# Norm scales in a two-block transformer on one core: roots and reciprocals in place of powers on GpSimd, and the weight splits around the feed-forward norms in another order

## The reference, cut to what matters

```python
def rmsnorm(x, g):
    return x * lax.rsqrt(jnp.mean(x * x, axis=-1, keepdims=True) + 1e-6) * g

def first_block(x, ...):                       # layer 0: attention, layer 1: recurrence
    for layer in range(2):
        h = rmsnorm(x, norm_mix_pre[layer])
        m = attention_mixer(h, ...) if layer % 2 == 0 else recurrent_mixer(h, ...)
        x = x + rmsnorm(m, norm_mix_post[layer])
        h = rmsnorm(x, norm_ffn_pre[layer])
        f = (silu(h @ w_gate[layer]) * (h @ w_up[layer])) @ w_down[layer]
        x = x + rmsnorm(f, norm_ffn_post[layer])

def second_block(x, ...):                      # no norm behind the sublayers
    h = h + dilated_diff_mixer(rms_norm(h, attn_norm), ...)
    h = h + swiglu_2(rms_norm(h, ffn_norm), ...)
    h = h + hgrn2_mixer(rms_norm(h, hgrn_norm), ...)
    h = h + moe_swiglu(rms_norm(h, moe_norm), ...)     # 8 experts, the best 2 per token
```

## Time and profile before

| | |
|---|---|
| median of 3 runs | 2200.21 us (2199.64 to 2201.91) |
| the profiled execution: its time, its span | 2202.57 us, 2200.8 us |
| TensorE busy | 2151.7 us, 98% of the span |
| VectorE, ScalarE, GpSimd busy | 1411.9, 1182.2, 43.6 us |
| mean granted TensorE clock | 0.99 of full speed |

### The profile page before, as it was taken

The page is one execution under the profiler, slowest core; times in us unless marked ns, Lnnn a source line. Parts: engine busy times, 40 slices in busy tenths (PEclk is TensorE's granted clock), DMA queues, the critical chain, the costliest instruction groups (busy, mean ns, idle before and its releaser), DMA issues.

```text
span 2200.8 us, 26591 instructions
## 1 busy us (share of the span) xinstructions
PE 2151.7 (98%) x10426; PEld 1754.3 (80%) x10426; DVE 1411.9 (64%) x1193; ACT 1182.2 (54%) x1107; POOL 43.6 (2%) x94
## 2 busy tenths in 40 slices
PE   7999999999999999999998999999999999999998
PEld 7757889868888758889876888888888888888887
DVE  1425444455444735542725888888888988888887
ACT  1335432444433534432533777767776777767775
POOL 1001000010000000000000000000000000000000
PEclk9999999999999999999997999999999999999999
DMA  7325554545554225555324999999999999999996
GB/s 251 115 77 191 190 183 149 186 172 191 190 174 144 96 77 201 191 185 162 123 96 156 359 347 361 370 338 374 340 363 350 358 347 360 371 337 374 341 363 256
DMA packets 208179, 539.60 MB, mean 245 GB/s; under 512 B 10045, under 2 KB 67486, under 8 KB 208110
## 3 DMA queue, kind: packets, MB, share of 16 engines
q1 hardware_dynamic: 204224, 530.61, 68.4%
q0 software_dynamic: 2096, 7.87, 1.1%
q10 hardware_dynamic: 1790, 0.14, 0.1%
HBM read 537.54 MB, written 1.05 MB: 245 GB/s over the span
## 4 chain that ended last, share of the span: by engine, by line
PE 90%; ACT 5%; issue 2%; DVE 2%; DMA 1%; POOL 1%; DVEq 0%; SPq 0%; ACTq 0%; POOLq 0%
PE ps L1962 12%; PE ps L1964 12%; PE ps L1963 12%; PE ps L509 11%; PE ps L622 5%; PE ps L624 5%; PE ps L623 5%; PE ps L586 5%; PE ps L527 4%; ACT ring_r L1953 3%; PE ps L663 3%; PE ps L665 3%; PE ps L664 3%; PE ps L1972 2%; PE ps L2017 1%
## 5 line engine op out<-in xcount | busy, mean ns | idle before, releaser
L1958 DVE TENSOR_TENSOR ring_r<-ring,ring_r 128x2048 fp32r<-128x2048 f32 x339 | 761.9, 2287 | 97.7 <-ACT ring_r L1953 97.7
L1953 ACT ACTIVATE ring_r<-ring 128x2048 fp32r<-128x2048 f32 x339 | 630.8, 1912 | 57.3 <-DMA ring<-in_moe_w_gate 46.5
L1962 PE MATMUL ps<-ring_r,arena_r 128*128 128x512 f32 x1344 | 532.2, 396 | 1.0 <-DVE arena_r L2190 1.0
L1964 PE MATMUL ps<-ring_r,arena_r 128*128 128x512 f32 x1344 | 524.9, 391 | 0.0
L1963 PE MATMUL ps<-ring_r,arena_r 128*128 128x512 f32 x1344 | 524.8, 391 | 0.0
L324 DVE TENSOR_TENSOR ring_r<-ring,ring_r 128x2048 fp32r<-128x2048 f32 x99 | 226.9, 2292 | 234.4 <-ACT ring_r L315 234.4
L1964 PEld LDWEIGHTS ps<-ring_r,arena_r 128*128 128x128 f32 x1344 | 253.0, 188 | 54.7
L1962 PEld LDWEIGHTS ps<-ring_r,arena_r 128*128 128x128 f32 x1344 | 253.2, 188 | 51.8 <-issue 1.2
L1963 PEld LDWEIGHTS ps<-ring_r,arena_r 128*128 128x128 f32 x1344 | 253.4, 189 | 50.4
L315 ACT ACTIVATE ring_r<-ring 128x2048 fp32r<-128x2048 f32 x99 | 189.4, 1917 | 182.1 <-DMA ring<-in_ffn_w_up 81.9
L509 PE MATMUL ps<-arena,ring 128*128 128x128 f32 (+1 forms) x1600 | 261.5, 324 | 4.3 <-ACT arena L368 2.7
(11 more groups left out here) (322 smaller groups left out, 1800.0 us busy)
## 6 DMA issues: line engine op xcount, KB each, us to landing
ring<-in_moe_w_gate SPq DMA_DIRECT2D x115, 1024.0 KB, 5.3
ring<-in_moe_w_up SPq DMA_DIRECT2D x112, 1024.0 KB, 5.3
ring<-in_moe_w_down SPq DMA_DIRECT2D x112, 1024.0 KB, 5.0
ring<-in_ffn_w_gate SPq DMA_DIRECT2D x33, 1024.0 KB, 5.1
ring<-in_ffn_w_up SPq DMA_DIRECT2D x33, 1024.0 KB, 5.2
ring<-in_ffn_w_down SPq DMA_DIRECT2D x33, 1024.0 KB, 4.9
ring<-in_attn_w_in SPq DMA_DIRECT2D x24, 1024.0 KB, 5.4
ring<-in_hgrn_w_in SPq DMA_DIRECT2D x16, 1024.0 KB, 5.5
```

The lines of the kernel that those rows point to most:

```text
L1953: nc.scalar.activation(unit_parts(k)[0], ring[:, slot_of(k), 0:2048], ACT.Copy).then_inc(m_hi, 1)
L1958: nc.vector.tensor_tensor(low, ring[:, slot_of(k), 0:2048], high, ALU.subtract).then_inc(m_lo, 1)
L1962: nc.tensor.matmul(out_, x[:, 0, f, :], w[0], start=first, stop=False)
L1964: return nc.tensor.matmul(out_, x[:, 0, f, :], w[1], start=False, stop=last)
```

## The change: who makes the scale, and where the weight splits stand

The powers on GpSimd (`norm_gpsimd`) are gone. ScalarE takes a square root behind its own sums (`ACT.Sqrt`, with epsilon as bias), and VectorE takes the reciprocal of it in front of the instruction that uses it; for the post norm VectorE also adds epsilon. A dummy root of one column (`sqrt_table`) stands at the head of each norm on ScalarE. In the feed-forward norms the splits stand in other places, and TensorE waits for each quarter of the turned tokens instead of for two at once.

```diff
@@ post_sums (ScalarE)
+            act.wait_ge(s_yse, 2 * (k - 1) + t + 1)
+            act.wait_ge(s_yss, 4 * (k - 1) + 2 * t + 2)
+            r = 16 + 2 * (k - 1) + t
+            nc.scalar.activation(rstd[:, r:r + 1], sumsq[:, c:c + 1], ACT.Sqrt, bias=sumsq[:, c - 1:c]).then_inc(s_yrt, 1)
@@ norm_sums (ScalarE)
+            c = 2 * k + t
+            act.wait_ge(s_ss, c + 1)
+            nc.scalar.activation(rstd[:, c:c + 1], sumsq[:, c:c + 1], ACT.Sqrt, bias=epscol[:, 0:1]).then_inc(s_rt, 1)
+        def sqrt_table(act):
+            nc.scalar.activation(rstd[:, 31:32], epscol[:, 1:2], ACT.Sqrt)
@@ norm_gpsimd, and its calls for k = 0 to 7
-        def norm_gpsimd(pool, step, k, t):
...
@@ post_gain (VectorE), behind the second piece
+                    nc.vector.tensor_scalar(sumsq[:, c:c + 1], sumsq[:, c:c + 1], EPS, None, ALU.add).then_inc(s_yse, 1)
@@ residual (VectorE)
+                dve.wait_ge(s_yrt, 2 * m + t + 1)
+                nc.vector.reciprocal(rstd[:, c:c + 1], rstd[:, c:c + 1]).then_inc(s_yrstd, 1)
@@ normalise_tokens (VectorE)
             dve.wait_ge(gpre_in, 16 * (k + 1))
+            dve.wait_ge(s_rt, c + 1)
+            nc.vector.reciprocal(rstd[:, c:c + 1], rstd[:, c:c + 1]).then_inc(s_rstd, 1)
@@ norm_scalar, ffn_norm_scalar, M_scalar: at the head
+            sqrt_table(act)
@@ ffn_norm_scalar
                 post_sums(act, k, 0)
+            highs_to(act, first + 1)
             norm_sums(act, k, 0)
             norm_high(act, k, 0)
-            highs_to(act, first + 2)
             if has_post(k):
                 post_sums(act, k, 1)
-                highs_to(act, first + 3)
-                norm_sums(act, k, 1)
-            else:
-                norm_sums(act, k, 1)
-                highs_to(act, first + 3)
+            highs_to(act, first + 2)
+            norm_sums(act, k, 1)
+            highs_to(act, first + 3)
             norm_high(act, k, 1)
@@ ffn_norm_vector
             residual(dve, k, 0)
+            lows_to(dve, first + 1)
             normalise_tokens(dve, k, 0)
             norm_low(dve, k, 0)
-            lows_to(dve, first + 1)
             if has_post(k):
                 post_gain(dve, k, 1)
                 lows_to(dve, first + 2)
                 residual(dve, k, 1)
-                lows_to(dve, first + 3)
-                normalise_tokens(dve, k, 1)
             else:
                 residual(dve, k, 1)
                 lows_to(dve, first + 2)
-                normalise_tokens(dve, k, 1)
-                lows_to(dve, first + 3)
+            normalise_tokens(dve, k, 1)
+            lows_to(dve, first + 3)
             norm_low(dve, k, 1)
@@ ffn_tensor
             k = 2 * n + 1
+            pe.wait_ge(s_htl, 4 * k + 1)
+            gate_tokens(0, 0, 0)
             pe.wait_ge(s_htl, 4 * k + 2)
-            gate_tokens(0, 0, 0), gate_tokens(0, 1, 0)
+            gate_tokens(0, 1, 0)
...
+            pe.wait_ge(s_htl, 4 * k + 3)
+            gate_tokens(0, 0, 1)
             pe.wait_ge(s_htl, 4 * k + 4)
-            gate_tokens(0, 0, 1), gate_tokens(0, 1, 1)
+            gate_tokens(0, 1, 1)
```

More of the change, by code:

```diff
@@ L169, in build @@
         ident_ok = sem("ident_ok")
+        eps_ok = sem("eps_ok")
         dist_ok = sem("dist_ok")
@@ L182, in build @@
         s_rstd = sem("s_rstd")
+        s_rt = sem("s_rt")
+        s_yrt = sem("s_yrt")
+        s_yse = sem("s_yse")
         s_xn = sem("s_xn")
@@ L400, in post_gain @@
                 nc.vector.tensor_tensor(XN[:, t, d], Y[:, t, d], gpost[:, d], ALU.mult).then_inc(s_yg, 1)
+                if h == 0:
+                    c = 16 + 4 * m + 2 * t
+                    nc.vector.tensor_scalar(sumsq[:, c:c + 1], sumsq[:, c:c + 1], EPS, None, ALU.add).then_inc(s_yse, 1)
         def residual(dve, k, t):
@@ L781, in setup_gpsimd_first @@
             step.link(nc.gpsimd.memset(halves[:, :], -0.5))
-            nc.gpsimd.memset(epscol[:, :], EPS)
+            nc.gpsimd.memset(epscol[:, :], EPS).then_inc(eps_ok, 1)
             step.link(nc.gpsimd.memset(ident[:, :], 0.0))
@@ L1004, in A_scalar @@
         def A_scalar(act, step):
+            act.wait_ge(eps_ok, 1)
             norm_scalar(act, 0)
@@ L2328, in _ @@
             pool.dma_start(gpost[:, :], row_of(*post_gains[0])).then_inc(gpost_in, 16)
-            norm_gpsimd(pool, step, 0, 0)
-            norm_gpsimd(pool, step, 0, 1)
             setup_gpsimd(pool, step)
@@ L2337, in _ @@
                     pool.dma_start(gpost[:, :], row_of(*post_gains[k - 1])).then_inc(gpost_in, 16)
-                norm_gpsimd(pool, step, k, 0)
-                norm_gpsimd(pool, step, k, 1)
                 if k == 2:
```

## The result

| | before | after |
|---|---|---|
| median of 5 runs | 2201.86 us (2199.64 to 2201.99) | 2212.86 us (2211.41 to 2218.31) |
| profiled execution: time, span | 2202.57, 2200.8 us | 2212.11, 2210.3 us |

A forecast was written before the change was run, and what follows sets the result against it. TensorE, busy 98% of the span, was taken as the bound. Terms -1.0 + 5.2 + 4.2 - 0.6 = +7.8 us, +11.1 with the clock fallen twice, gave 2211.3 us; own range 2208.5 to 2215, wider range 2203.5 to 2216.

The forecast's parts named there:

- k = 3: Feed-forward norm 3: copy of g1 waits for its load and holds up square and normalising; +5.2 us, clock apart.
- k = 5: Feed-forward norm 5: the same wait for g1's load, without sums of Y; +4.2 us, clock apart.
- k = 1: Feed-forward norm 1: g1 has landed long before, second half of up starts sooner; -1.0 us.
- k = 7: Norm 7: reciprocal and normalising follow VectorE's subtraction at once, without GpSimd's two steps; -0.6 us.
- The scale: Norm scales: root on ScalarE and reciprocal on VectorE replace GpSimd's 1.17 us route, gaining 0.6 to 0.7 us each.
- rival 2: Norms: the wait for the scale is the whole story, g1's copies hold up nothing; -3.6 us, 2196.6 us; chance 0.06.
- Table loads at nothing: ScalarE: seven more table loads of 1.28 us each stand ahead of waits and cost nothing.
- The clock falls at k = 3 and 5: TensorE's clock falls to half in both 3.7 us waits, slowing the last output unit by 1.66 us each, +3.3.
- Rival 1: TensorE's clock holds at k = 3 and 5: 2208.0 us, or 2209.7 if it falls once; chance 0.24.
- Rivals 2 and 3: The latter: waits at k = 3 and 5 half as long, gains offset the rest, within 0.2%, 2203.5 us; chance 0.10.
- rival 4: ScalarE: table loads start only after their root's wait, 9 us in all, 2220 us; chance 0.08 with other trouble above 2216.
- Rival 5: New scale gains nothing, so k = 1 and 7 lose their gains: 2212.9 us; chance 0.52 together with the forecast.

The follow-up runs named there:

- experiment 3: Changed kernel, but at k = 3 and 5 copy and subtraction of g1 stand behind the tokens' high and low parts again: 2204.11 us, 1.001 of before.
- experiment 2: Kernel before with GpSimd's powers kept, but splits and TensorE's quarter waits in the new order: 2216.63 us, 1.0066 of before.
- experiment 1: Kernel before with only the new scales (roots, reciprocals, dummy roots); splits and TensorE's waits in the old order: 2197.26 us against 2201.65, ratio 0.9978.
- 9: New scales, quarter waits and old split order, except g1's split goes ahead at k = 1 only: 2194.51 us against 2201.35 before, ratio 0.997.
- 8: New scales and old split order, with TensorE's quarter waits as in the changed kernel: 2197.22 us against 2200.11 before, ratio 0.9985.
- experiment 5: Changed kernel, but u0's copy stands ahead of the sums of Y of t = 1 again: 2207.78 us, 1.003 of before.
- experiment 6: Changed kernel without the dummy roots, so the first real root of each norm loads the table: 2220.39 us, 1.008 of before.
- experiment 4: Changed kernel, but at k = 3 and 5 only g1's subtraction on VectorE goes behind; ScalarE's copy stays ahead: 2210.27 us, 1.0035 of before.
- experiment 10: Kernel 9 plus unread filling products in the routing's waits; the second kernel has more of them: 2189.23 us (0.9946 of before) and 2187.84 us (0.9938).

## Why the prediction was right

The time came out 1.6 us above the forecast of 2211.3, and against before in the same runs at +11.0 where +11.1 was put down. The mechanism is the one forecast: experiment 3 takes away the wait for g1's load and most of the loss goes. That the totals meet within 0.1 us is luck: by the means the loss is 13.3 us, and in the profile the four norms lose 9.6 us and not 11.1, while E adds 2.3 that no step had. Step by step, with the profile:

- **k = 3, +5.2 and 1.66 for the clock: 6.9 forecast, 6.7 measured.** The load landed 5.0 us after its issue (5.1 taken), TensorE waited 3.31 us (3.7), the last output unit took 5.25 us (5.26). Up to its end the loss is 5.5, with t = 1 another 1.2 (5.8 and 1.1 by the forecast's own steps).
- **k = 5, +4.2 and 1.66: 5.9 forecast, 4.7 measured.** The wait was 3.42 us (3.7), and the clock cost 1.3 (transposes and last output unit took 1.97 and 4.25 us and not 1.32 and 3.60). Another 0.4 us come back at the start of the up with u1, where TensorE made a short stop in before (0.12 us of idling) and makes none in the others, experiment 2 without the new scales included; the forecast had left it out.
- **k = 1, -1.0: measured -1.1. k = 7, -0.6: measured -0.7.** Both are right as nets. But k = 1 is the difference of two larger sizes that I did not see apart: the scales gain 2.1 us (experiment 1) and g1 ahead another 1.7 (9 against 8), while t = 1's order takes 2.7 of it back (9 against after), 1.2 by u0's place and 1.5 by u1's (experiment 5).
- **The scale, 0.6 to 0.7 us each: right for t = 1, too high for t = 0, where it is 0.5.** From the end of the read-out (447.67 + 0.19) to the residual at 448.56 the new route takes 0.70 us against 1.17. The gain put down needs 0.5 us for the whole route, so only 0.1 for hand-offs beside 0.21 for the root and 0.17 for the reciprocal; the root takes 0.30, the reciprocal 0.16 and the hand-offs 0.24. (Read as 0.5 us of hand-offs alone, the forecast's figures would give a gain of 0.3.) With t = 1 VectorE had idled 0.93 us (experiment 1's row) and 0.83 ahead of its two uses of GpSimd's scales, since GpSimd's adds took 2.14 and 1.01 us there, and now spends 0.2 on a reciprocal instead: 0.7 and 0.6 us. So the forecast's "not much more to gain" held for one scale, but two lie one behind the other in that chain: 1.5 us at k = 3, 1.5 at k = 1 (2.1 with t = 0) and 4.4 in all with the old order, where rival 2, without g1's wait, asked for 3.6.
- **Table loads at nothing: right,** and by experiment 6 only because the dummy root pulls them forward.
- **The clock falls at k = 3 and 5: right,** but E took 2.3 us more than before, with the clock at half for longer, which no step had. Nothing in E was changed; other kernels show -0.6 to +1.1 there. What sets it is open.
- **Rival 1 (clock holds)** is what experiment 4's profile shows for a wait of 2.50 us. **Rivals 2 and 3** fell on the wait itself, **rival 4** on the loads that sit in idle time. **Rival 5** gave 2212.9, nearer to the measured 2212.86 than the forecast, so the time does not speak against it; experiment 1 does, where the new scale gains 4.4 us.

What the forecast did not price is the share of t = 1. u0's copy behind the sums of Y costs 3.6 us by the stages and 4.6 by the medians (experiment 5); in the forecast its 1.1 us at k = 3 was only a remainder. Taking parts away one by one gives 8.5 for g1 and 4.6 for u0, more than the 11.0 of both, for they cover each other: with g1's wait gone, t = 1's waits show in full (1.79 + 0.95 + 1.76 us in experiment 3), while in after the wait for u0 is 0.61.

## What to carry to other kernels

An engine's queue has one order, so a copy that waits for a load holds up everything written behind it: put a split ahead of a chain only where its data is there by then, stage by stage (here at k = 1, not at k = 3 and 5). A table load costs nothing if a dummy call pulls it into idle time, and up to 1.3 us if the first real call brings it, as here at k = 1, besides what the clock does behind it. Where small products and short waits alternate on TensorE, price the clock beside the waits: filling the routing's gaps with products that nobody reads gave 4.0 and 6.7 us (experiment 10's two kernels and 9, each against before beside it), as much as all the new scales (4.4) or more.

## What the hardware showed that was not expected

- One product of two fp32 128x128 tiles is two instructions: 28 products gave x56 and 6.41 us, 0.23 us for a product. The transposes stay one instruction each (x8 for eight).
- Falls of the clock differ from run to run of one kernel. The five runs of after lie 7 us apart at mean clocks of 0.987 to 0.991, those of before 2.4.
- A fall behind a wait of 3.3 to 3.4 us cost 1.7 us at k = 3 and 1.3 at k = 5 in after; waits of 2.96 us (k = 1, before) and 2.50 (k = 3, experiment 4) left the clock up, and so did stops of 1.75 us in after; in other kernels it fell in such stops.
- In the routing the clock is at half for most of the stretch below in after (0.57), and for none of it with the gaps filled (1.00 in experiment 10's second kernel). That kernel runs 42 products more and is 6 to 7 us faster for it.

```profile
1180.00:1212.00 32.00, 22.59 (x97) 19.90 (x96) 20.69 (x44) 13.91 (x14) 0.00 (x0) 0.57 0.32 124
```
